# A delta-rule chunk stage: whole PSUM products copied by one engine each, in place of halves by two

## The reference, cut to what matters

```python
def step(s, inp):
    r_t, w_t, k_t, v_t, kk_t, a_t = inp
    s_kk = jnp.einsum('bhvk,bhk->bhv', s, kk_t)
    s = (s * w_t[:, :, None, :]
         - s_kk[..., None] * (kk_t * a_t)[:, :, None, :]
         + v_t[..., None] * k_t[:, :, None, :])
    return s, jnp.einsum('bhvk,bhk->bhv', s, r_t)
```

## Time and profile before

| | |
|---|---|
| median of 3 runs | 3174.72 us (3170.84 to 3177.66) |
| the profiled execution | 3179.57 us, span 3177.9 us |
| busy, share of the span | TensorE 88%, VectorE 59%, ScalarE 40%, GpSimd 6% |
| mean granted TensorE clock | 0.918 of 2.4 GHz |
| chunk stage | 223.19 to 420.27 us of the span, 4 pairs of some 48 us |

### The profile page before, as it was taken

How to read it: one execution, slowest core, us unless ns; L and a number is a source line. 1 busy time by engine, 2 the same in 40 slices (tenths; PEclk the granted TensorE clock), 3 DMA queues, 4 the chain that set the end, 5 groups by cost and what they waited for, 6 DMA issues and landing times.

```text
span 3177.9 us, 60570 instructions
## 1 busy us (share of the span) xinstructions
PE 2808.2 (88%) x22131; PEld 2554.7 (80%) x22131; DVE 1870.6 (59%) x3518; ACT 1274.2 (40%) x2578; POOL 179.9 (6%) x245
## 2 busy tenths in 40 slices
PE   6947668999999999986579999966899999999998
PEld 5636657899999999974467888851689999999998
DVE  2267753798998555532434444461179889955554
ACT  1223311346776444421123444420024577744443
POOL 0013300000000000000001111113000000000000
PEclk9868869999999999988669999986799999999999
DMA  4300002454444555552002112215235444445554
GB/s 153 122 19 23 16 12 100 140 179 153 156 158 147 183 180 179 182 191 97 0 1 60 57 57 57 59 54 172 73 127 182 157 155 158 156 166 182 178 182 136
DMA packets 112356, 378.02 MB, mean 119 GB/s; under 512 B 14569, under 2 KB 24042, under 8 KB 111538
## 3 DMA queue, kind: packets, MB, share of 16 engines
q1 hardware_dynamic: 88562, 322.17, 30.5%
q0 software_dynamic: 13248, 43.98, 4.6%
q10 hardware_dynamic: 10368, 9.44, 1.0%
HBM read 371.52 MB, written 4.01 MB: 118 GB/s over the span
## 4 chain that ended last, share of the span: by engine, by line
PE 54%; issue 32%; DVE 10%; ACT 2%; DMA 1%; ACTq 1%; POOLq 0%; DVEq 0%; SPq 0%; POOL 0%
PE ps L705 53%; DVE arena L1238 3%; ACT arena L1894 2%; DVE arena L1242 1%; DVE arena L1626 1%; DMA arena<-in_cache_n 0%; PE ps L742 0%; DVE arena L1621 0%; ACTq L533 0%; PE ps L961 0%; PE ps L967 0%; DVE arena L1614 0%; DVE arena L1252 0%; ACTq L534 0%; DVE arena L1758 0%
## 5 line engine op out<-in xcount | busy, mean ns | idle before, releaser
L1238 DVE TENSOR_TENSOR ring_lo<-ring,w_hi 128x1024 fp32r<-128x1024 f32 x512 | 625.3, 1223 | 422.9 <-ACT w_hi L1894 419.6
L1894 ACT ACTIVATE arena<-ps 128x264 f32<-128x264 f32 (+18 forms) x1021 | 412.4, 423 | 987.6 <-PE ps L705 837.0
L1894 ACT ACTIVATE w_hi<-ring 128x1024 fp32r<-128x1024 f32 x512 | 541.9, 1059 | 393.8 <-PE ps L705 393.4
L705 PE MATMUL ps<-arena 64*64 64x64 f32 (+11 forms) x5228 | 515.8, 283 | 164.6 <-DVEq L1235 60.1
L705 PEld LDWEIGHTS ps<-arena 64*64 64x64 f32 (+6 forms) x5228 | 402.6, 166 | 283.1 <-DMA arena<-in_cache_n 56.8
L705 PE MATMUL ps<-x_hi,w_hi 128*128 128x264 f32 x2048 | 596.8, 291 | 15.5 <-DVE ring_lo L1238 15.5
L705 PE MATMUL ps<-h_hi,w_hi 128*128 128x264 f32 x2048 | 581.7, 284 | 6.8 <-DVE ring_lo L1238 6.8
L705 PE MATMUL ps<-x_hi,ring_lo 128*128 128x264 f32 x2048 | 586.0, 286 | 0.0
L705 PE MATMUL ps<-x_lo,w_hi 128*128 128x264 f32 x2048 | 585.9, 286 | 0.0
L705 PE MATMUL ps<-h_lo,w_hi 128*128 128x264 f32 x2048 | 583.8, 285 | 0.0
L705 PE MATMUL ps<-h_hi,ring_lo 128*128 128x264 f32 x2048 | 583.3, 285 | 0.0
(11 more groups left out here) (161 smaller groups left out, 2357.6 us busy)
## 6 DMA issues: line engine op xcount, KB each, us to landing
ring<-in_wstream SPq DMA_DIRECT2D x608, 512.0 KB, 3.3
arena<-in_cache_t POOLq DMA_DIRECT2D x128, 192.0 KB, 2.6
arena<-in_cache_n ACTq DMA_DIRECT2D x72, 128.0 KB, 2.5
arena<-in_cache_n POOLq DMA_DIRECT2D x56, 128.0 KB, 2.8
arena<-in_mla_w POOLq DMA_DIRECT2D x1, 3072.0 KB, 10.3
arena<-in_state POOLq DMA_DIRECT2D x4, 512.0 KB, 4.6
out_wkv_s<-arena POOLq DMA_DIRECT2D x4, 512.0 KB, 4.1
arena<-in_consts SPq DMA_DIRECT2D x1, 1408.0 KB
```

The source lines that it names most:

```text
L705: return nc.tensor.matmul(out, lhsT, rhs, start=start, stop=stop, **kw)
L1238: return v.tensor_tensor(out, a, b, op)
L1894: return nc.scalar.activation(out, in_, func, **kw)
```

## The change

Each of the 128-partition products is copied by one engine over all partitions. ScalarE takes all of RHS, XT, Z and `nWU`; VectorE takes all of X. TensorE raises one semaphore per product instead of one per half, and waits for one count instead of two. VectorE loses its `begin`, `level_z` and `solve`, and keeps `chunk_rows`, X, the masked products, the sample sums and `chunk_maps`. Its first sample sum now comes after both X copies of level 1, its second after level 4. In `begin`, TensorE makes XT before X.

```diff
 # TensorE
             def begin(x):
...
-                        if q == 3:
-                            last.then_inc(half_done[f], 1)
-                take(6 + x, 2)
-                take(2 + x, 2)
+                last.then_inc(for_act, 1)
+                take(6 + x)
+                take(2 + x)
                 w.next(nt_ready[x])
+                for f in range(2):
+                    mm(ps[par[f], 2 + x, 0:256], eye[f], eye4[f], stop=True, skip_group_check=True)
+                for f in range(2):
+                    last = nc.tensor.matmul(ps[par[f], 2 + x, 0:256], eye[f], NTl[x][0][par[f], :], **acc)
+                last.then_inc(for_act, 1)
...
+                last.then_inc(for_dve, 1)
...
             def level_z(x, lev):
-                w.next(x_ready[x], 2)
-                take(4 + x, 2)
+                w.next(x_ready[x])
+                take(4 + x)
...
+                last.then_inc(for_act, 1)
             def level_x(x, lev):
-                w.next(z_ready[x], 2)
-                w.next(xt_ready[x], 2)
+                w.next(z_ready[x])
+                w.next(xt_ready[x])
...
 # VectorE
-            def level_z(x):
+            def level_x(x, lev):
                 w.next(for_dve)
-                own(v.tensor_copy(Zs[x][hi], ps[hi, 4 + x, 0:256]))
-                tell(z_ready[x], bank_free[4 + x])
...
-                w.next(for_dve)
-                own(v.tensor_copy(XTs[x][hi], ps[hi, 2 + x, 0:256]))
-                tell(xt_ready[x])
+                own(v.tensor_copy(Xs[x], ps[:, 6 + x, 0:256]))
+                tell(x_ready[x])
+                if lev == 4:
+                    tell(bank_free[6 + x])
                 if lev + 2 < 6:
                     tt(q4(NTl[x][lev % 2]), q4(LT[x]), mask(2 + lev + 2), ALU.mult).then_inc(nt_ready[x], 1)
...
-            def solve(x):
-                w.next(for_dve)
-                own(v.tensor_scalar(nWU[x][hi], ps[hi, x, :], -1.0, None, ALU.mult))
-                tell(nwu_ready[x], bank_free[x])
...
-                for x in range(2):
-                    begin(x)
-                for lev in range(1, 6):
+                for lev in range(5):
                     for x in range(2):
-                        level_z(x)
+                        level_x(x, lev)
                     if lev == 1:
                         sample_sums(c)
-                    for x in range(2):
-                        level_x(x, lev)
-                for x in range(2):
-                    solve(x)
                 sample_sums(c + 1)
 # ScalarE
             def level_z(x):
                 w.next(for_act)
-                own(fn(Zs[x][lo], ps[lo, 4 + x, 0:256]))
+                own(fn(Zs[x], ps[:, 4 + x, 0:256]))
                 tell(z_ready[x], bank_free[4 + x])
             def level_x(x, lev):
-                if lev < 5:
-                    w.next(for_act)
-                    own(fn(Xs[x][lo], ps[lo, 6 + x, 0:256]))
-                    tell(x_ready[x])
...
                 w.next(for_act)
-                own(fn(XTs[x][lo], ps[lo, 2 + x, 0:256]))
+                own(fn(XTs[x], ps[:, 2 + x, 0:256]))
                 tell(xt_ready[x])
...
-                own(fn(q4(RHS[x])[lo, :, 64:128], q4(ps[lo, x, 0:256])))
+                own(fn(q4(RHS[x])[:, :, 64:128], q4(ps[:, x, 0:256])))
...
-                own(fn(nWU[x][lo], ps[lo, x, :], ACT.Copy, scale=-1.0))
+                own(fn(nWU[x], ps[:, x, :], ACT.Copy, scale=-1.0))
```

More of the change, by code:

```diff
@@ L886, in _ @@
             eye4 = [eye[f].unsqueeze(1).broadcast_to([CH, 4, CH]) for f in range(2)]
-            half_done = (for_act, for_dve)
             def chunk_products(c):
@@ L917, in begin @@
                 w.next(ab_ready)
-                take(x, 2)
+                take(x)
                 for q in range(4):
@@ L933, in begin @@
                                                 eye[f], **acc)
-                        if q == 3:
-                            last.then_inc(half_done[f], 1)
-                for f in range(2):
-                    mm(ps[par[f], 2 + x, 0:256], eye[f], eye4[f], stop=True, skip_group_check=True)
-                for f in range(2):
-                    nc.tensor.matmul(ps[par[f], 2 + x, 0:256], eye[f], NTl[x][0][par[f], :], **acc
-                                     ).then_inc(half_done[f], 1)
+                last.then_inc(for_dve, 1)
             def level_z(x, lev):
                 w.next(nt_ready[x])
-                w.next(x_ready[x], 2)
-                take(4 + x, 2)
+                w.next(x_ready[x])
+                take(4 + x)
                 for q in range(4):
@@ L968, in level_x @@
                                                 q4(Zs[x])[par[f], q, :], q4(XTs[x])[par[f], q, :], **acc)
-                        if q == 3:
-                            last.then_inc(half_done[f], 1)
+                last.then_inc(for_act, 1)
             def solve(x):
-                w.next(xt_ready[x], 2)
-                w.next(rhs_ready[x], 2)
-                take(x, 2)
+                w.next(xt_ready[x])
+                w.next(rhs_ready[x])
+                take(x)
                 for q in range(4):
@@ L979, in solve @@
                         last = mm(ps[par[f], x, q * P:(q + 1) * P], q4(XTs[x])[par[f], q, :], q4(RHS[x])[par[f], q, :])
-                        if q == 3:
-                            last.then_inc(half_done[f], 1)
+                last.then_inc(for_act, 1)
             def chunk_maps(x):
                 w.next(rows_dve)
-                w.next(nwu_ready[x], 2)
+                w.next(nwu_ready[x])
                 take(4)
@@ L1588, in mask2 @@
                 return wm[:, m, :].unsqueeze(1).unsqueeze(1).broadcast_to([P, 2, 2, CH])
-            hi = par[1]
             def chunk_rows(x):
@@ L1609, in chunk_rows @@
                 tell(ab_ready, bank_free[4], bank_free[5])
-            def level_z(x):
+            def level_x(x, lev):
                 w.next(for_dve)
-                own(v.tensor_copy(Zs[x][hi], ps[hi, 4 + x, 0:256]))
-                tell(z_ready[x], bank_free[4 + x])
-            def level_x(x, lev):
-                if lev < 5:
-                    w.next(for_dve)
-                    own(v.tensor_copy(Xs[x][hi], ps[hi, 6 + x, 0:256]))
-                    tell(x_ready[x])
-                    if lev == 4:
-                        tell(bank_free[6 + x])
-                w.next(for_dve)
-                own(v.tensor_copy(XTs[x][hi], ps[hi, 2 + x, 0:256]))
-                tell(xt_ready[x])
+                own(v.tensor_copy(Xs[x], ps[:, 6 + x, 0:256]))
+                tell(x_ready[x])
+                if lev == 4:
+                    tell(bank_free[6 + x])
                 if lev + 2 < 6:
                     tt(q4(NTl[x][lev % 2]), q4(LT[x]), mask(2 + lev + 2), ALU.mult).then_inc(nt_ready[x], 1)
-                if lev == 5:
-                    tell(bank_free[2 + x])
-            def begin(x):
-                w.next(for_dve)
-                own(v.tensor_copy(q4(RHS[x])[hi, :, 64:128], q4(ps[hi, x, 0:256])))
-                tell(rhs_ready[x], bank_free[x])
-                level_x(x, 0)
-            def solve(x):
-                w.next(for_dve)
-                own(v.tensor_scalar(nWU[x][hi], ps[hi, x, :], -1.0, None, ALU.mult))
-                tell(nwu_ready[x], bank_free[x])
             def chunk_maps(c):
@@ L2060, in _ @@
             fn(Bb, cum[1], ACT.Exp, scale=-1.0).then_inc(e_ready, 1)
-            lo = par[0]
             def chunk_rows(x):
```

## The result

| | before | changed |
|---|---|---|
| time, median of 4 runs each | 3172.78 us (3159.48 to 3177.66) | 3132.74 us (3125.47 to 3138.31) |
| ratio | | 0.9879, 95% interval 0.984 to 0.9918 |
| profiled execution | 3179.57 us | 3138.31 us, span 3136.7, clock 0.924 |
| chunk stage in the trace, from VectorE's first BK copy to the end of the last map copy | 196.73 us | 151.94 us |
| rest of the span | 2981.2 us | 2984.8 us |

The kernel is faster by 1.2%: 40.0 us by the medians, where 44 were forecast; 3132.7 against a predicted 3131. In the two traces the stage is 44.8 us shorter and the part outside it 3.6 us longer. The second figure means little: over the twelve traces of this study the part outside the stage lies between 2970 and 2985 us, whatever the kernel.

What follows compares the result with a forecast made beforehand. VectorE's instruction count times pitch was taken to bound the chunk-stage levels: 10.40 us a pair there plus 0.65 at the maps, 11.05, times four pairs 44.2 us, giving 3131 us (ratio 0.986), bounds 3124 to 3139, 8-in-10 range 3115 to 3155.

Steps and rivals of the forecast that it cites:

- The chain and its price: Chunk stage: VectorE's instruction count times 0.57 us pitch sets levels 1 to 5; an operation's price doesn't depend on partitions.
- The new level: Chunk stage levels: a free level takes 3.12 us, TensorE-bound but for 0.33; level 1 3.19, level 5 to solve copy 3.64.
- ScalarE's hand-over: From ScalarE's copy end to TensorE's product: taken as 0.17 us; bounds 0.11 to 0.4, -1.5 to +5.5 us over the stage.
- The masked products: VectorE in levels 2 and 3: 1.30 us each beside GpSimd, 0.43 otherwise, making levels 3 and 4 last 3.70 and 3.82 us.
- The far bound: Masked products each held for a whole GpSimd operation, 2.41 us: some 1.1 us longer, 18 us over the stage.
- The first rival: TensorE's granted clock stays low in the levels: 3149 us if half are cold, up to 3168 for all; chance 0.15.
- more is gained: Half-clock stretches run at full, maps about 1 us, some masked products fast: 2 to 4 us a pair more, 3115 to 3124; chance 0.12.
- likeliest case: The layout as worked out, 3131 us with its own range of 3124 to 3139; chance 0.66.
- The sums: VectorE's sample sums: first hidden but for 0.06 of 1.22 us, second hidden after level 4 with 1.8 us of cover.
- Slower by ScalarE's serial copies: ScalarE's queued copies become the chain if their pitch passes 1.39 us; at 1.5 us, 3183 us; chance 0.03.
- No change: Something hidden, GpSimd or the weights' stream, holds the pair, or a later stage gives the time back: 3172 us; chance 0.04.
- GpSimd's state load: The next pair's load has less time but lands well before that pair's first sum, so it costs nothing.

Runs made afterwards that it cites:

- e3: The changed kernel with ScalarE's Z and XT copies each made as two instructions of 64 partitions, both on ScalarE: 3141.75 us, 0.9915 of the kernel before.
- e1: The kernel before with Z alone copied whole by ScalarE, all other halves kept: 3149.29 us, 0.9939 of the kernel before.
- e6: The changed kernel's whole copies with engines swapped, VectorE taking RHS, Z, XT and the solve, ScalarE X alone: 3154.42 us, 0.9944 of the kernel before.
- e4: The changed kernel with GpSimd's five operations after the first sum working on 1 of 16 rows: 3116.8 us, 0.9821 of the kernel before.
- e5: The changed kernel with LT also copied to PSUM by ScalarE, where masked products of levels 0 to 3 read it: 3123.31 us, 0.9841 of the kernel before.
- e0: The changed kernel run again without an edit, beside the kernel before: 3126.32 us, 0.9858 of the kernel before.
- e7: e5 with the second block's maps moved to banks 6 and 7: 3124.16 us, 0.9859 of the kernel before.
- e8: e7 with the masked products of `chunk_rows` also reading from PSUM banks: 3116.07 us, 0.9816 of the kernel before.
- e9: e7 with state loads of quarters 2 and 3 and stores of 0 to 2 cut to 64 of 1024 columns: 3115.76 us, one execution.

## Why the prediction was right, point by point

**The chain and its price: right.** The step "an operation's price doesn't depend on the number of partitions" carries the result. e3 shows it by undoing it: the same data in twice the instructions makes levels of 4.00 us and 9 to 12 us more of stage. e1 shows that VectorE's queue is what the removed Z copies were paid in. But "VectorE's number of instructions times their pitch" holds for the level that it was read from. Before it, the first X products of levels 1 to 3 stand 7.40 and 6.96 us apart (289.07, 296.47 and 303.43), with the sum in the first stretch, held masked products in both, and TensorE at half speed in the second. The forecast took the old levels as the measured 27.87 us, so it doesn't hang on that rule. How the 10 us a pair divide among fewer copies, the hidden sum and the clock that rose was not separated.

**The new level: right.** Levels 1 and 2 were laid out as 3.19 and 3.12 us and took 3.17 and 3.14 (274.61, 277.78, 280.92); level 5 to the solve copy 3.64 against 3.60. TensorE's waits of 16 times and 19.6 us for VectorE's queue before X products are gone: 0.4 us is left before L957.

ScalarE's hand-over was taken as 0.17 us from a row of another stage; it is about 0.1 (Z's copy of 278.52 to 278.90, product at 279.00), the lower of the bounds. VectorE was expected to be busy 23 us in a pair and was 24.66: the four masked products beside GpSimd took 7.28 us where they had taken 5.05.

**The masked products: the term that was mis-sized.** The step reads "a masked product takes 0.43 us, but 1.30 us while GpSimd works", and I stayed with the one row at 1.30. The far bound, "each be held for a whole operation of GpSimd", had the mechanism right but not the size: each was longer than 1.30 us by 0.26 to 0.71 and not by 1.1. The masked product takes until 0.28 us after the end of the GpSimd operation that it meets: 1.56 to 2.01 us in the new order, 2.54 in e6. The 1.30 wasn't a duration of that operation but a distance to the next end, and in an order with another phase it means nothing. The earlier trace rows gave it beside L625 and L629, and not beside L626, which it met. Levels 3 and 4 took 4.06 and 4.53 us against 3.70 and 3.82: 1.07 us in pair two, and its levels 18.50 against 17.47. e4 takes GpSimd's length away and e5 its conflict; both give back 7 to 11 us of stage. By the excess over free levels, (4.06 + 4.53 - 2 x 3.12) x 4 = 9.4 us was due.

**The clock: what offset it.** The first rival, that the clock stays low, fell for the levels: these windows of TensorE in pair two's levels 3 and 4 and through the stretches around them are at 1.00, with waits of 0.9 to 1.4 us in them (columns as in the earlier trace rows).

```profile
274.60:280.90 6.30, 6.05 (x199) 1.00 0.01 3
280.90:289.50 8.60, 6.30 (x200) 1.00 0.02 4
289.50:295.50 6.00, 5.98 (x195) 1.00 0.43 122
```

The argument against that rival had a slip in it: levels busy 2.8 of 3.8 us (0.74) are not denser than the stretch that kept 1.00 (11.38 of 14, 0.81). The second window above, busy 0.73, was granted 1.00 all the same. In e0 the clock did fall in `begin`, ahead of the levels.

A part of "more is gained" came true instead, and at the size given for it, "about 1 us for the maps". In the kernel before, the second block's maps ran from 319.52 for 2.84 us at half speed (0.51 from 319.3 to 322.5 us); now they take 1.98 us at 1.00 (the last row of the timeline above). Outside the levels, pair two took 18.97 us where 48.45 - 27.87 - 0.65 = 19.93 were forecast. So +1.03 and -0.96 nearly cancel, and the pair gained 10.98 us where 11.05 were forecast. The sum was right partly by this luck; each term alone would have moved the forecast by 4 us, within the likeliest case's range of 3124 to 3139. The luck is also that of the execution: in e0's trace the levels are the same, but the rest of pair two takes 20.57 us, and the pair gained 9.40.

**The sums: right.** The first runs beside TensorE's Z products (278.46). The second waits 1.24 us for GpSimd and is done by 292.48, 3.06 us before the first map copy at 295.54; the cover was put at 1.8 us. In e5 GpSimd ends no earlier against a shorter pair and the sum waits 3.7 us, which the pair still hides.

**The other rivals.** Slower by ScalarE's serial copies: no; ScalarE's pitch is 0.50 us, and four are 2.0 us under TensorE's 2.8. e3 shows what it is like when that queue does decide. No change: no; the interval of the ratio lies below 1, and no later stage gave the time back. GpSimd's state load does come late now: L622 waits three times and 9.2 us in all for it, but nobody waits for L622 in this order.

## What to carry to other kernels

Where a chain of small products is bounded by an engine's queue, count instructions and not elements: halving a 256-column copy over two engines cost two full copies here. Then see which engine has its turn beside GpSimd, and keep that one short: e6, with the same copies merged but on VectorE, gave only a third of the gain. A duration read beside another engine's work is a distance to that engine's next end: compare the ends before it is carried into a new order, and give a VectorE operation with two SBUF inputs one operand in PSUM if it must run there.

## What the runs showed of the hardware

A VectorE tensor-tensor operation on 128 x 256 fp32 with both inputs in SBUF takes 0.42 us alone. Where it starts inside a GpSimd tensor-tensor operation, it ends 0.27 to 0.30 us after that operation's end, in before, in the changed kernel, in e3, e6 and e7 alike, and so takes up to 2.57 us. Where it starts first, it isn't held: in before one ran 0.42 us from 225.67 and GpSimd's L622 from 225.69, and there L622 took 2.64 us where others take 2.34. With one input in PSUM it takes 0.42 us beside the same operations. The same instructions after the same waits had a granted clock of 1.00 in one execution of the changed kernel and of 0.51 in the other. The stops of TensorE of 0.5 to 2.6 us without a recorded releaser, behind the same records in e7, e8 and e9, were not expected and are not explained.
